# A four-layer-stage encoder trunk on one core: residual stream and closing projections laid out by tokens, with the norm edge worked tile by tile

## What is computed

```python
for i in range(DEPTH):                       # DEPTH = 2
    mod = c_act @ ada_w[i] + ada_b[i]        # 6 vectors: shift, scale, gate, twice
    h = rms_norm(x, sandwich_g[i, 0]) * (1 + sc_m) + sh_m
    y = mla_mixer(h, ...) if i % 2 == 0 else gdn_mixer(h, ...)      # both end in  o @ w_o
    x = x + gt_m * rms_norm(y, sandwich_g[i, 1])
    h = rms_norm(x, sandwich_g[i, 2]) * (1 + sc_f) + sh_f
    y = jnp.square(jax.nn.relu(h @ ffn_w1[i])) @ ffn_w2[i]
    x = x + gt_f * rms_norm(y, sandwich_g[i, 3])
```

## Time and profile before

| | |
|---|---|
| times of three runs | 1556.16, 1540.58, 1556.4 us; median 1556.16 us |
| the profiled execution: span from first to last instruction | 1546.3 us (its only time that is given) |
| PE busy | 1466.5 us, 95%, 6911 matmuls |
| DVE, ACT, POOL busy | 870.7 us (56%), 525.6 us (34%), 76.0 us (5%) |
| mean granted TensorE clock | 0.939 |
| DMA | 166.05 MB, mean 107 GB/s |

### The profile page before, as it was taken

How to read it: one execution, slowest core, us unless ns; L and a number is a source line. 1 busy time by engine, 2 the same in 40 slices (tenths; PEclk the granted TensorE clock), 3 DMA queues, 4 the chain that set the end, 5 groups by cost and what they waited for, 6 DMA issues and landing times. The chain is left out here.

```text
span 1546.3 us, 17806 instructions
## 1 busy us (share of the span) xinstructions
PE 1466.5 (95%) x6911; PEld 1190.5 (77%) x6911; DVE 870.7 (56%) x1425; ACT 525.6 (34%) x678; POOL 76.0 (5%) x73
## 2 busy tenths in 40 slices
PE   7988999799999999998999899999989999999997
PEld 7866667678888888876888788788777888888885
DVE  5869675777776776736567635223445434343343
ACT  4523433253132222324676401132435223141331
POOL 0000001100000000020001300002110000000011
PEclk9989999879999999996999979599979999999997
DMA  8634202515656556413133221102221232323211
GB/s 271 177 103 152 82 1 82 190 55 185 197 163 211 170 186 195 134 58 110 55 103 89 55 68 55 55 28 110 64 72 55 82 100 91 102 88 93 98 55 55
DMA packets 173701, 166.05 MB, mean 107 GB/s; under 512 B 22574, under 2 KB 169148, under 8 KB 173372
## 3 DMA queue, kind: packets, MB, share of 16 engines
q1 hardware_dynamic: 171452, 164.92, 33.7%
q10 hardware_dynamic: 2176, 0.13, 0.1%
HBM read 157.96 MB, written 7.08 MB: 107 GB/s over the span
## 5 line engine op out<-in xcount | busy, mean ns | idle before, releaser
L148 DVE TENSOR_TENSOR w_lo<-w_raw,w_hi 128x2048 fp32r<-128x2048 f32 (+1 forms) x97 | 221.2, 2280 | 107.4 <-ACT w_hi L143 107.2
L143 ACT ACTIVATE w_hi<-w_raw 128x2048 fp32r<-128x2048 f32 (+1 forms) x97 | 182.1, 1877 | 243.7 <-PE bank L155 231.6
L153 PE MATMUL bank<-h_hi_mlp,w_lo 128*128 128x512 f32 x512 | 206.3, 403 | 6.2 <-DVE h_lo_mlp L358 6.2
L153 PE MATMUL bank<-mlp_u_hi,w_lo 128*128 128x512 f32 x512 | 204.6, 400 | 0.0
L155 PE MATMUL bank<-h_hi_mlp,w_hi 128*128 128x512 f32 x512 | 203.5, 397 | 0.0
L154 PE MATMUL bank<-h_lo_mlp,w_hi 128*128 128x512 f32 x512 | 203.1, 397 | 0.0
L154 PE MATMUL bank<-mlp_u_lo,w_hi 128*128 128x512 f32 x512 | 201.6, 394 | 0.0
L155 PE MATMUL bank<-mlp_u_hi,w_hi 128*128 128x512 f32 x512 | 201.6, 394 | 0.0
L278 DVE SCALAR_TENSOR_TENSOR ada_acc<-ada_raw,c_act,ada_acc 128x256 f32<-128x256 f32 x280 | 138.7, 495 | 10.0
L153 PE MATMUL bank<-h_hi_gdn,w_lo 128*128 128x512 f32 x320 | 142.5, 445 | 0.0
L154 PE MATMUL bank<-h_lo_gdn,w_hi 128*128 128x512 f32 x320 | 131.3, 410 | 0.0
(11 more groups left out here) (306 smaller groups left out, 2126.8 us busy)
## 6 DMA issues: line engine op xcount, KB each, us to landing
w_raw<-in_ffn_w SPq DMA_DIRECT2D x64, 1024.0 KB, 5.7
ada_raw<-in_ada_w SPq DMA_DIRECT2D x44, 1024.0 KB, 5.3
w_raw<-in_gdn_w_in SPq DMA_DIRECT2D x16, 1024.0 KB, 5.8
w_raw<-in_mla_w_o SPq DMA_DIRECT2D x4, 1024.0 KB, 6.5
w_raw<-in_gdn_w_o SPq DMA_DIRECT2D x4, 1024.0 KB, 5.3
y<-in_x SPq DMA_DIRECT2D x1, 2048.0 KB, 7.7
v_tok<-in_ada_w SPq DMA_DIRECT2D x2, 1024.0 KB, 12.5
y<-in_ada_w SPq DMA_DIRECT2D x2, 1024.0 KB, 7.1
```

The lines of the kernel that those rows point to most:

```text
L143: act.activation(w_hi[n % 2][:, 0:size[n]], w_raw[n % 2][:, 0:size[n]], ACT.Copy).then_inc(w_hi_ready, 1)
L148: dve.tensor_tensor(w_lo[n % 2][:, 0:size[n]], w_raw[n % 2][:, 0:size[n]], w_hi[n % 2][:, 0:size[n]].bitcast(F32), ALU.subtract).then_inc( ...
L153: pe.matmul(ps, s_lo, m_hi, start=first, stop=False)
```

## The change

- `x` and `y` lie by tokens: 128 partitions are 128 tokens, `x[:, t]` is tile t of 4 with all 1024 features. The sums of the norms then run along the free dimension and come out of ACT's square itself (`accum_out`).
- The closing projections (w_o of both mixers, w2) have the activation stationary and 512 columns of weights moving. Their chunks are 512 rows by 512 columns; chunks c = 0, 1 give the left half of y for the 4 token tiles, c = 2, 3 the right half. Four PSUM banks hold the four tiles. Chunks 0 and 1 are worked chunk by chunk; the last two are worked tile by tile (`close_last`), so both must be ready together: the weights get a third pair of buffers.
- Beside `close_last` runs the edge, tile by tile: `square_last` and root on ACT, gate, inverse and add on DVE (in the MLPs the gate multiply is POOL's), `square_next` on ACT, `scale_next` on DVE, turn on PE (`turn_tile`), modulate and round by halves on ACT and DVE (`round_tile`, `rest_tile`). The gate is turned and copied to all partitions once per edge.
- The next sub-layer's first chunk is worked by halves of 256 tokens (`first_half`) between the turns.
- GDN's input and output chunks keep two weight buffers (`buffer`); MLA's closing and the MLPs rotate through three. The hardware loops of the MLP are gone. The ada blocks 15 to 18 move into attention, one 128x256 instruction per item.
- At the start, x is squared by tokens on ACT, scaled on DVE (four instructions of 128x1024) and only then turned. The two small blocks' projection of GDN follows its first tiles instead of being interleaved.
- At the end each token tile of x is stored as it is ready, 512 KB each, without a turn.

```diff
+    closing = [1, 4, 0, 4]
+    group, last_group = [2] * 4 + [1, 4, 1, 4], [2] * 4 + closing
+    mlp = group * 3 + last_group
+    tiles = [2] * 3 + [3] * 4 + [8] * 2 + closing + mlp + [2] * 16 + closing + mlp
     parts = [1] * 2 + [3] + [4] * 4 + [1] * (len(size) - 7)
-    return size, tiles, parts
+    tiles_to = [sum(tiles[:n]) for n in range(len(tiles) + 1)]
+    spent = [tiles_to[n + 1 + (tiles[n] == 0)] for n in range(len(tiles))]
+    buffer = [n % 2 for n in range(9)] + [(1, 0, 2)[n % 3] for n in range(36)] + [(1, 0)[n % 2] for n in range(20)]
+    buffer += [(2, 1, 0)[n % 3] for n in range(32)]
+    before = [max([m for m in range(n) if buffer[m] == buffer[n]], default=None) for n in range(len(buffer))]
...
+        def hi_of(n):
+            return w_hi[buffer[n]] if buffer[n] < 2 else third[n >= N_GDN][0]
...
+            if before[n] is not None:
+                act.wait_ge(tile_done, spent[before[n]])
...
+        def closing_src(w, c):
+
+            rows_at, cols_at = 512 * (c % 2), 512 * (c // 2)
+            return rows(w[rows_at:rows_at + 512, cols_at:cols_at + 512], 4)
...
+        def close_chunk(pe, t, c, n, s_hi, s_lo, ps, rests=None):
+            hi, lo = w_views(n, 4)
+            for kk in range(4):
+                k = 4 * (c % 2) + kk
+                if rests:
+                    pe.wait_ge(rests[0], rests[1] + k + 1)
+                last = product(pe, ps, s_hi[:, k, tokens(t)], s_lo[:, k, tokens(t)], hi[:, kk], lo[:, kk],
+                               c % 2 == 0 and kk == 0, c % 2 == 1 and kk == 3)
+            return last
+
+        def turn_tile(pe, e, t, ring):
+            pe.wait_ge(xn_ready, TT * e.at + t + 1)
+            for i in range(2):
+                r = 2 * t + i
+                if r >= 3:
+                    pe.wait_ge(hf_dve if (r - 3) % 2 else hf_act, TT * e.at + (r - 3) // 2 + 1)
+                for j in range(4):
+                    k = 4 * i + j
+                    last = pe.transpose(ring[r % 3][:, P * j:P * j + P], e.xn[t % 2][:, P * k:P * k + P], ident)
+                last.then_inc(xn_turned, 1)
+
+        def close_last(pe, e, n, s_hi, s_lo, into, ring, half_free, first):
+
+            pe.wait_ge(w_lo_ready, n + 3)
+            for t in range(TT):
+                half_free(pe, t)
+                close_chunk(pe, t, 2, n + 2, s_hi, s_lo, into[t][:])
+                if first and t >= 2:
+                    turn_tile(pe, e, t - 2, ring)
+                if t == 0:
+                    pe.wait_ge(w_lo_ready, n + 4)
+                close_chunk(pe, t, 3, n + 3, s_hi, s_lo, into[t][:]).then_inc(tile_done, 1)
+            if first:
+                pe.wait_ge(w_lo_ready, n + 5)
+                pe.wait_ge(h_tile, TT * e.at + 2)
+                first(pe, 0, 0)
+                turn_tile(pe, e, 2, ring)
+                first(pe, 0, 1)
+                turn_tile(pe, e, 3, ring)
+                pe.wait_ge(h_tile, TT * e.at + 4)
+                first(pe, 1, 0).then_inc(tile_done, 1)
+                first(pe, 1, 1).then_inc(tile_done, 1)
+
+        def first_half(pe, n, half, i, ps, h_hi, h_lo):
+            hi, lo = w_views(n, KD)
+            cols, tok = slice(P * i, P * i + P), slice(256 * half, 256 * half + 256)
...
+        def square_last(act, e, t, src):
+            act.wait_ge(half_biased, e.at + 1)
+            act.activation(sq[0], src, ACT.Square, accum_out=column(LAST_SQ, t)).then_inc(y_squared, 1)
+            act.wait_ge(y_squared, TT * e.at + t + 1)
+            act.activation(column(Y_ROOT, t), column(LAST_SQ, t), ACT.Sqrt, bias=column(BIAS, t),
+                           scale=1 / D).then_inc(y_root, 1)
+
+        def square_next(act, e, t):
+            act.wait_ge(x_new, TT * e.at + t + 1)
+            act.activation(flat(sq_both), x[:, t], ACT.Square, accum_out=column(X_SQ, t)).then_inc(x_squared, 1)
+            act.wait_ge(x_squared, TT * e.at + t + 1)
+            act.activation(column(X_ROOT, t), column(X_SQ, t), ACT.Sqrt, bias=bias_t[:, 0:1], scale=1 / D).then_inc(x_root, 1)
+
+        def round_tile(act, e, t, ring):
+            l, s = e.nxt
+            at = TT * e.at + t
+            act.wait_ge(xn_turned, 2 * at + 1)
+            act.wait_ge(factors_ready, 3 + 2 * e.at)
+            if t:
+                act.wait_ge(h_tile, at)
+            for k in range(4):
+                last = act.activation(e.hf[:, k], ring[2 * t % 3][:, P * k:P * k + P], ACT.Identity,
+                                      bias=section(l, s)[:, k:k + 1], scale=section(l, s + 1)[:, k:k + 1])
+            last.then_inc(hf_act, 1)
+            act.wait_ge(hf_act, at + 1)
+            act.activation(e.h_hi[:, 0:4, tokens(t)], e.hf[:, 0:4], ACT.Copy).then_inc(hi_act, 1)
+            act.wait_ge(hf_dve, at + 1)
+            act.activation(e.h_hi[:, 4:8, tokens(t)], e.hf[:, 4:8], ACT.Copy).then_inc(hi_act, 1)
+
+        def edge_act(act, e, src, ready, ring):
+            for t in range(TT):
+                ready(act, t)
+                square_last(act, e, t, src(t))
+                if e.nxt:
+                    square_next(act, e, t)
+                    if t:
+                        round_tile(act, e, t - 1, ring)
+            if e.nxt:
+                round_tile(act, e, TT - 1, ring)
+
+        def add_to_x(dve, e, t):
+            at = TT * e.at + t
+            dve.wait_ge(y_root, at + 1)
+            dve.reciprocal(column(Y_INV, t), column(Y_ROOT, t)).then_inc(y_inv, 1)
+            dve.wait_ge(y_inv, at + 1)
+            dve.wait_ge(gated_first, at + 1)
+            dve.wait_ge(gated_last, at + 1)
+            dve.scalar_tensor_tensor(x[:, t], y[:, t], column(Y_INV, t), x[:, t], ALU.mult, ALU.add).then_inc(x_new, 1)
+
+        def scale_next(dve, e, t):
+            at = TT * e.at + t
+            dve.wait_ge(x_root, at + 1)
+            dve.reciprocal(column(X_INV, t), column(X_ROOT, t)).then_inc(x_inv, 1)
+            dve.wait_ge(x_inv, at + 1)
+            if t >= 2:
+                dve.wait_ge(xn_turned, 2 * at - 2)
+            dve.tensor_scalar(e.xn[t % 2][:], x[:, t], column(X_INV, t), None, ALU.mult).then_inc(xn_ready, 1)
+
+        def rest_tile(dve, e, t, ring):
+            l, s = e.nxt
+            at = TT * e.at + t
+            dve.wait_ge(xn_turned, 2 * at + 2)
+            dve.wait_ge(factors_ready, 3 + 2 * e.at)
+            if t:
+                dve.wait_ge(h_tile, at)
+            for k in range(4, 8):
+                last = dve.tensor_scalar(e.hf[:, k], ring[(2 * t + 1) % 3][:, P * (k - 4):P * (k - 3)],
+                                         section(l, s + 1)[:, k:k + 1], section(l, s)[:, k:k + 1], ALU.mult, ALU.add)
+            last.then_inc(hf_dve, 1)
+            for i in range(2):
+                ks = slice(4 * i, 4 * i + 4)
+                dve.wait_ge(hi_act, 2 * at + i + 1)
+                last = dve.tensor_tensor(e.h_lo[:, ks, tokens(t)], e.hf[:, ks], e.h_hi[:, ks, tokens(t)].bitcast(F32),
+                                         ALU.subtract)
+            last.then_inc(h_tile, 1)
+
+        def edge_dve(dve, e, take, ring):
+            for t in range(TT):
+                take(dve, t)
+                add_to_x(dve, e, t)
+                if e.nxt:
+                    scale_next(dve, e, t)
+                    if t:
+                        rest_tile(dve, e, t - 1, ring)
+            if e.nxt:
+                rest_tile(dve, e, TT - 1, ring)
+        ha_stack = root.enter_context(ExitStack())
...
-                sp.dma_start(x_tok, a["x"][0].rearrange("(t p) d -> p t d", p=P)).then_inc(x_in, 16)
+                for t in range(TT):
+                    sp.dma_start(x[:, t], a["x"][0, P * t:P * t + P, :]).then_inc(x_in[t], 16)
                 sp.dma_start(pos_i, a["positions"].to_broadcast([P, SEQ])).then_inc(pos_in, 16)
...
+                pe.wait_ge(first_scaled, TT)
+                for k in range(KD):
+                    if k >= 4:
+                        pe.wait_ge(x_copied, k - 3)
+                    for t in range(TT):
+                        last = pe.transpose(bank[k % 4][:, P * t:P * t + P], y[:, t, P * k:P * k + P], ident)
...
+                dve.wait_ge(first_root, 1)
+                dve.reciprocal(norms[:, X_INV], norms[:, X_ROOT]).then_inc(first_inv, 1)
+                dve.wait_ge(first_inv, 1)
+                for t in range(TT):
+                    dve.tensor_scalar(y[:, t], x[:, t], column(X_INV, t), None, ALU.mult).then_inc(first_scaled, 1)
...
+                for m in ADA_ATTENTION:
+                    load_ada(sp, m + 2)
...
+                    if i and i % KD == 0 and i <= N:
+                        ada_reduce(pe, ADA_ATTENTION[i // KD - 1])
...
+                    if i > KD and i % KD == 1:
+                        ada_finish(dve, ADA_ATTENTION[i // KD - 1])
+                    if i < N:
+                        ada_multiply_row(dve, ADA_ATTENTION[i // KD], i % KD)
...
+            def close_act(act):
+                round_weights(act, n0 + 1)
```

(70 more changed lines are left out.)

2214 lines of the change are left out of this document (1082 added, 1132 removed).

## The result

| | before | changed |
|---|---|---|
| median of four runs | 1555.78 us | 1482.83 us |
| lowest and highest | 1540.58, 1556.4 us | 1479.31, 1491.33 us |
| span of the profiled execution | 1546.3 us | 1481.7 us |
| mean granted clock in it | 0.939 | 0.956 |

The ratio of the times is 0.957, with a 95% interval of 0.9515 to 0.9625: the change makes the kernel 4.3% faster. The predicted 1495.0 us was 12 us too slow. By span, with which the sum was made, the forecast was 1489.2 and the result 1481.7.

The account below looks back on a forecast made before the run. PE's stream bounds the MLPs; edges cost 118.0 us and would cost 55.0. -63.0 + 6 (attention) - 3.3 (projection) + 3.2 (start) = -57.1: span 1489.2, from the median 1499.1, taken as 1495; 8-in-10 range 1474 to 1524.

Parts of the forecast that it names:

- The price of the edges before: The four stretches between sub-layers and at the end cost 34.0 + 30.8 + 30.3 + 22.9 = 118.0 us, lower clock included.
- Start: Before the first product: scaling x delays its turns and the ada blocks queued behind, +3.2 us, bounds 0 and 5.
- edge 3: End of the kernel: one tile's chain and one store after the last product's start, 7.9 us.
- The MLA projection: Output projection after attention loses PE's wait for ada sums, the 3.8 us one less remainder: -3.3 us.
- Edge 0: MLA closing into MLP 0: transposes 4.2, PE idle 4.2, gate turn 1.0, halves 1.3; 10.7 us in all.
- Edge 1: MLP 0 into GDN: PE waits 10.2, added PE work 6.5, lower clock 3; 19.7 us in all.
- Edge 2: GDN closing into MLP 1: idle 4.2, PE work 6.5, two-buffer stall about 5, clock 1; 16.7 us in all.
- Attention: Ada rows added to DVE in attention partly fill its wait for scores: +6 us, bounds 3 and 18.
- B: Rival: added work hides in attention, start, transposes and halves, edge 1 a third shorter; -15 us, 1480; chance 0.15.
- A: Rival: the edges' chains bind harder through in-order waits, dear halves, lower clock; 8 us more per edge, 1520; chance 0.22.
- C: Rival: activation-stationary products cost more in a dense stream; slower by 1% from +0.038 each, 1591 at +0.05; chance 0.05.
- D: Rival: MLP hand-offs cost PE about 7 us in each of eight groups, using up the gain; 1550; chance 0.08.

Follow-up runs that it names:

- experiment 3: Changed kernel, but no tile's chain at an edge begins before the last tile's closing is done: 1546.9 us, ratio 1.0036 to the kernel before.
- experiment 2: Changed kernel with DVE's inverse root and four scalings of x ahead of all angle steps but two: 1480.4 us, ratio 0.959 to the kernel before.

## Why the prediction was right, and where it was off

The mechanism was right. The gain is that of the edges, experiment 3 shows that it is the overlap, and the account adds to -64.6 us of span where -57.1 were forecast. That edges 0 to 2 gained 51.1 us together, for 51.3 forecast, is luck: edge 1 gained 7.0 more, edges 0 and 2 gained 1.9 and 5.3 less. The other 7.5 us are attention (3.7 better), GDN (3.3 better) and terms of 1.4 us and less. By its steps:

- **The price of the edges before**, 118.0 us, stands. **Start** (+3.1 for +3.2) and **edge 3** (7.1 for 7.9) came as worked out. The mechanism named for the start was incomplete: the scaling is late not only by its own time (2.7 us) but because the angle steps stand before it in DVE's queue, from 13.7 to 22.4 us, which experiment 2 took away.
- **A 256-column product** was taken as 0.13 and measures 0.121: 96 of them cost 0.4 us more than 48 of 512, not 1.3. (Within a run they follow each other in 0.118, half of a product of 512.) The floor by the Trainium skill (TensorE: Matmul & The Clock Gate, section LDWEIGHTS), 0.107 each, lies 12% lower; that the weight load and not the 256 columns sets the pace is not shown. A turn of eight took 0.8 us, not 1.05. Over one edge, with the gate's turn, both terms were 2.1 us too dear.
- **The MLA projection** lost the wait for modulation sums, as forecast, but not the one that the forecast read. The 3.8 us wait of the earlier trace rows ended at 134.0, in the low-rank projections, and the changed kernel has it too (3.8 us, ending at 137.3). What the projection lost is one of 3.0 us for DVE's last addition to a block (L294). That the -3.3 came out near is luck.
- **Edge 0.** Extra waits of 5.9 us (the two start distances, 2.84 and 3.43, less a pitch each) against 4.2: 1.7 too few, since the last tile's h comes 13.7 us after PE's last closing product (298.01 to 311.66), not 12.2. And 2.4 us of clock, counted as nothing; the second profile of the same kernel had none.
- **Edge 1** gained 7.0 more than forecast, the largest miss. 3.1 of it, at the forecast's price (2.4 as measured), is only where the line was drawn: turning the gate and tiles 0 and 1 was charged to the edge, but lies before the last closing product, in MLP 0's stretch. The step that failed is the wait: the brackets give 8.0 us, not 10.2. Tile 0 was not 2.1 us late, and PE never waited before its first turn there; the DVE cycle of 8.3 us was right, it measures 8.55. The rest is 0.9 us for the halves, 0.5 for the two turns left, and 0.6 because the edge cost 31.4 us before (48.3 less 72 products at 0.234), not 30.8. The 3 us of clock were right: two pieces at the lower level, from 679.6 to 682.5 and from 692.8 to 696.2, lost half their 6.3 us.
- **Edge 2** gained 5.3 less. The stall by the two weight buffers was foreseen in its place and size (4.9, measured 5.08). The term mis-sized is the clock: 1 us in the forecast, and three pieces at the lower level that lost 6.0. 2.6 of it lies behind the stall and 3.4 behind the two waits for h, where the forecast had none. These waits were also 1.8 us longer than the 4.2 forecast, as at edge 0, which the cheaper turns and halves made up.
- **Attention** came out of its own bounds: +2.3, with bounds of 3 and 18. DVE's added work was 14.0 us (70.54 less 56.55), not 18, and its waiting for scores fell from 15.0 us to 4.1, so that 10.9 of the 14.0 went into it:

```profile
DVE bank L993 <- PE bank L954: 4.1, 8, 1.3
```

  Adding rows just before a wait fills that wait; I discounted this by half without a row that said so.
- **GDN** (-3.3, with bounds of -2 and +3) is put down to clock, as the two windows above show for a larger case: the same code took 346.7 and 350.2 us in two profiles, and the change touches nothing in it.
- **POOL beside DVE**, for which the prediction names up to 2 us an edge, met nothing to test it: at edge 1 only DVE's reciprocal of 0.16 us runs beside one of POOL's multiplications of the right half, and each of these takes 1.28 or 1.29 us.
- **From span to median** the allowance of 5.8 us was too large: the changed kernel's median is 1.1 above its profiled span.

Of the rivals, B (attention at +3, start at 0, transposes and halves at their floors, edge 1 a third shorter) is closest to what happened, at 1480: attention and the halves came so, edge 1 a fifth shorter (15.7 of 19.7, with what lies in MLP 0's stretch), the start not. A is out: its 8 us more an edge did not come; edges 0 and 2 exceeded the forecast by 1.9 and 5.3, mostly in clock. C is out: MLP 1's window shows 1498 matmuls in 346.00 us, 0.231 each, with the same closing products in it. D is out: the MLPs changed by +1.4 and -1.4 us; one wait of 0.8 us for DVE's y (L1261) is all that the hand-offs leave in MLP 0.

The signs named in advance held, but for attention (79.7, not near 83), PE's waits at edge 0 (5.6, not 4) and edge 1 (8, not 10) and edge 0's 21.9 us from the last closing product to the second chunk instead of 20.

## What to carry to other kernels

Where a norm stands between two matmul stages, lay the closing product out so that its output tile holds whole rows of the norm, and let each tile's chain run beside the next tile's products: here all of the gain is in that overlap, and none in the layout by itself. Then walk each in-order queue for what stands ahead of the chain's instructions (a weight's rest that waits for a buffer, a block of side work, angle steps), because one such instruction stops PE, and the clock that drops behind the stop costs more (2.6 us behind a stop of 5.5 here). Added side work belongs just ahead of a wait that the engine has anyway: the same four blocks cost 2.3 us in attention and 20.7 in the closing, put there in two lots.

## What the runs showed of the hardware

- The GDN stage, with the same instructions, took 329.2 to 356.3 us in the profiles, and 364.5 in that of experiment 2; in the two windows shown only the granted clock differs (0.98 and 0.91), for 21 us. Here that is 1.4% of the whole, as large as most single edits. DVE's, ACT's and POOL's busy times agree within 1.3 us in them. Two profiles of one kernel's code stand 3.5 us apart there.
- A wait of PE of 5.1 us in a dense stream was followed by 5.3 us in which the 13 products that ran were at the lower clock level (0.50), a loss of 2.6 us. Waits of 2.4 and 3.2 us were followed by a low clock in some executions (edge 0 at 0.95) and not in others (1.00).
- Products with a weight tile stationary and 256 columns of an activation moving take 0.121 us each in a run of 24, half of the 0.234 of 512 columns. The closing products, with the activation stationary and 512 columns of weights moving, follow each other as before: MLP 1 has both kinds, 0.231 us each.
